# Differential attention inside a decoder layer: queries and keys transposed by VectorE in 32x32 blocks, and two of each head's steps in other slots

## What is computed

```python
h = x @ w_in                                   # all projections, q, k, v of both branches and the gates
dq, dk, dv, dz, db, da, aq, ak, av, ga, gb = jnp.split(h, split_at, axis=-1)
# differential attention, per head and block of 128 queries
s = einsum('bhmqd,bhmkd->bhmqk', qb, kb) * 64 ** -0.5 + alibi_bias     # m = 0, 1
p = softmax(s)
p_diff = p[:, :, 0] - lam * p[:, :, 1]
o = rms_norm(p_diff @ v, norm_w) * (1 - lambda_init)
```

## Time and profile before

| | us |
|---|---|
| median of 3 runs (lowest, highest) | 1954.68 (1954.41, 1956.05) |
| profiled execution, time | 1955.3 |
| its span in the profile | 1953.4 |
| TensorE busy | 1938.1 (99%) |
| VectorE busy | 1287.9 (66%) |
| ScalarE busy | 934.6 (48%) |

### The profile page before, as it was taken

The page is one execution under the profiler, slowest core; times in us unless marked ns, Lnnn a source line. Parts: engine busy times, 40 slices in busy tenths (PEclk is TensorE's granted clock), DMA queues, the critical chain, the costliest instruction groups (busy, mean ns, idle before and its releaser), DMA issues.

```text
span 1953.4 us, 33127 instructions
## 1 busy us (share of the span) xinstructions
PE 1938.1 (99%) x11260; PEld 1593.1 (82%) x11260; DVE 1287.9 (66%) x1873; ACT 934.6 (48%) x1286; POOL 43.1 (2%) x104
## 2 busy tenths in 40 slices
PE   9999999999999999999999999999999999999997
PEld 7788887888888888887888888788888888888886
DVE  7768577676557575757567656577775466664656
ACT  5555465554445555555544435644443444443442
POOL 0102010010100000000000000000000000000000
PEclk9999999999999999999999999999999999999999
DMA  7444444444554545454655676555555556555554
GB/s 259 159 141 152 153 140 142 151 152 140 173 183 163 182 161 182 158 183 156 199 190 197 212 238 212 172 191 196 194 192 195 191 194 192 192 195 192 195 191 173
DMA packets 98012, 353.19 MB, mean 181 GB/s; under 512 B 10832, under 2 KB 11120, under 8 KB 97776
## 3 DMA queue, kind: packets, MB, share of 16 engines
q1 hardware_dynamic: 97904, 351.65, 54.5%
HBM read 349.51 MB, written 2.10 MB: 180 GB/s over the span
## 4 chain that ended last, share of the span: by engine, by line
PE 96%; DVE 1%; ACT 1%; issue 1%; DMA 0%; SPq 0%; DVEq 0%; ACTq 0%
PE pg L393 88%; PE B L393 5%; DVE gates L1235 1%; PE B L491 0%; DMA raw<-in_weights 0%; PE B L649 0%; PE B L670 0%; PE B L582 0%; DVE wlo L1227 0%; ACT whi L827 0%; DVE cT L1235 0%; ACT hraw L1112 0%; PE B L523 0%; ACT gates L1100 0%; PE B L685 0%
## 5 line engine op out<-in xcount | busy, mean ns | idle before, releaser
L1227 DVE TENSOR_TENSOR wlo<-raw,whi 128x1024 fp32r<-128x1024 f32 (+1 forms) x640 | 778.3, 1220 | 520.1 <-ACT whi L827 502.9
L827 ACT ACTIVATE whi<-raw 128x1024 fp32r<-128x1024 f32 (+1 forms) x640 | 673.7, 1056 | 669.8 <-PE pg L393 661.1
L393 PE MATMUL pg<-whi,act_x 128*128 128x512 f32 x2960 | 957.5, 396 | 1.3 <-ACT whi L827 0.9
L393 PEld LDWEIGHTS pg<-whi,act_x 128*128 128x128 f32 x2960 | 555.9, 188 | 123.7 <-issue 8.5
L393 PE MATMUL pg<-wlo,act_x 128*128 128x512 f32 x1480 | 574.7, 390 | 0.0
L393 PE MATMUL pg<-whi,act_a 128*128 128x512 f32 x1632 | 505.0, 389 | 0.5 <-DVE act_a L1227 0.5
L393 PEld LDWEIGHTS pg<-whi,act_a 128*128 128x128 f32 x1632 | 306.4, 188 | 64.8 <-DVE act_a L1227 1.4
L393 PEld LDWEIGHTS pg<-wlo,act_x 128*128 128x128 f32 x1480 | 278.4, 188 | 52.9
L393 PE MATMUL pg<-wlo,act_a 128*128 128x512 f32 x816 | 317.5, 389 | 0.0
L393 PEld LDWEIGHTS pg<-wlo,act_a 128*128 128x128 f32 x816 | 153.2, 188 | 31.6
L393 PE MATMUL pg<-whi,act_b 128*128 128x512 f32 x512 | 158.5, 389 | 0.0
(11 more groups left out here) (227 smaller groups left out, 1025.7 us busy)
## 6 DMA issues: line engine op xcount, KB each, us to landing
raw<-in_weights SPq DMA_DIRECT2D x646, 512.0 KB, 3.8
gates<-in_ln_in SPq DMA_DIRECT2D x4, 512.0 KB, 6.4
gates<-in_ln_in SPq DMA_DIRECT2D x1, 2048.0 KB, 8.1
out<-gates SPq DMA_DIRECT2D x8, 256.0 KB, 2.7
raw<-in_weights SPq DMA_DIRECT2D x4, 256.0 KB, 4.5
cT<-in_xT SPq DMA_DIRECT2D x2, 512.0 KB, 7.6
qT<-in_xrow SPq DMA_DIRECT2D x2, 512.0 KB, 6.2
kT<-in_xrow SPq DMA_DIRECT2D x2, 512.0 KB, 5.4
```

The lines of the kernel that those rows point to most:

```text
L393: return nc.tensor.matmul(o, l, r, start=start, stop=stop)
L827: return nc.scalar.activation(o, i, ACT.Copy, scale=scale)
L1227: return V.tensor_tensor(o, a, b, op)
```

## The change

VectorE turns queries and keys: 16 block transposes for each, straight from `hraw` to `qT` or `kT` in SBUF, a few in each slot (4, 2, 4, 4, 2 in slots 19 to 23 for q and 3, 2, 3, 3, 3, 2 in slots 24 to 29 for k in a loop body; two in each of slots 8 to 23 in the first body). TensorE's transposes L649 and ScalarE's copies from `B[0]` are gone, and the factor 1/8 goes into the copy of q out of PSUM. The semaphore `dve_qkT` takes the place of `pe_qkT` and `act_qkT`: ScalarE's copy of the k group to `hraw` now waits until VectorE has turned the whole of q. The products with v move from s0+5 to slots 6, 12, 18 and 23, which for the first three heads is the slot of the next head's scores and ahead of them; the output transposes move from s0+7 to slots 10, 16, 22 and 25, which for the first three is the slot of the next head's probability transposes, behind them.

```diff
-DA_TURN = [(21, 23), (27, 29)]
-DA_TURN_FIRST = [(10, 12), (18, 20)]
+DA_TURN = [{19: 4, 20: 2, 21: 4, 22: 4, 23: 2}, {24: 3, 25: 2, 26: 3, 27: 3, 28: 3, 29: 2}]
+DA_TURN_FIRST = [{s: 2 for s in range(8, 16)}, {s: 2 for s in range(16, 24)}]
 HEAD_SLOTS = [0, 6, 12, 18]
+PV_SLOTS = [6, 12, 18, 23]
+OT2_SLOTS = [10, 16, 22, 25]
...
@@ TensorE
-            def da_turn(j, which, half, e, first):
...
-                        last = nc.tensor.transpose(B[0][:, i * SEQ + t * P:i * SEQ + (t + 1) * P],
-                                                   hraw[:, t, h * P:(h + 1) * P], ident)
-                last.then_inc(N["pe_qkT"], 1)
...
+            def da_mix(j, s):
+                for h, s0 in enumerate(HEAD_SLOTS):
+                    if s == PV_SLOTS[h]:
+                        pe.wait_ge(N["act_pT"], 1 + HB * j + h + 1)
+                        mm(B[3][:, 0:P], pT[:, 0:P], vda[:, 0, h * P:(h + 1) * P])
...
                 for h, s0 in enumerate(HEAD_SLOTS):
                     if s == s0:
-                        pe.wait_ge(N["act_qkT"], 1 + 4 * j + 4)
+                        pe.wait_ge(N["dve_qkT"], 1 + 2 * j + 2)
...
-                    if s == s0 + 5:
-                        pe.wait_ge(N["act_pT"], 1 + HB * j + h + 1)
...
-                    if s == s0 + 7:
-                        if h == HB - 1 and turning:
-                            pe.wait_ge(N["act_qkT"], 1 + 4 * (j + 1) + 2)
+                for h in range(HB):
+                    if s == OT2_SLOTS[h]:
                         pe.wait_ge(N["dve_oh2"], 1 + HB * j + h + 1)
...
@@ ScalarE
-            def rows_out(pair, dst, func=ACT.Copy):
+            def rows_out(pair, dst, func=ACT.Copy, scale=1.0):
...
                 if what == "q":
                     act.wait_ge(N["pe_conv"], 1 + 6 * NB)
-                    act.wait_ge(N["pe_qkT"], 1 + 4 * j)
-                    rows_out(i % 2, lambda t: hraw[:, t, :])
+                    act.wait_ge(N["dve_qkT"], 1 + 2 * j)
+                    rows_out(i % 2, lambda t: hraw[:, t, :], scale=CH ** -0.5)
                 if what == "k":
-                    act.wait_ge(N["pe_qkT"], 1 + 4 * j + 2)
+                    act.wait_ge(N["dve_qkT"], 1 + 2 * j + 1)
                     rows_out(i % 2, lambda t: hraw[:, t, :])
...
-            def da_turns(j, s, first):
...
-                        copy((qT, kT)[which][:, 2 * half:2 * half + 2, :],
-                             B[0][:, :].rearrange("p (h s) -> p h s", h=2), CH ** -0.5 if which == 0 else 1.0
-                             ).then_inc(N["act_qkT"], 1)
...
@@ VectorE
-                    if s == s0 + 5:
+                for h in range(HB):
+                    if s == PV_SLOTS[h]:
                         dve.wait_ge(N["act_oss"], 1 + HB * j + h + 1)
...
-                    if s == s0 + 7:
+                    if s == OT2_SLOTS[h]:
                         dve.wait_ge(N["act_oT2"], 1 + HB * j + h + 1)
...
+            def da_turns(j, s, first):
+                for which, slots in enumerate(DA_TURN_FIRST if first else DA_TURN):
+                    if s not in slots:
+                        continue
+                    at = sum(n for k, n in slots.items() if k < s)
+                    if at == 0:
+                        g = which if first else which + 1
+                        dve.wait_ge(evac[g % 2], 2 * NB + 2 * j + g // 2 + 1)
+                        dve.wait_ge(N["pe_s"], 1 + HB * j)
+                    out = blocks_out((qT, kT)[which][:, :, :])
+                    for i in range(at, at + slots[s]):
+                        a, b = divmod(i, 4)
+                        ins = V.transpose(out[b * SB:(b + 1) * SB, :, :, a, :], blocks_in[a * SB:(a + 1) * SB, :, :, b, :])
+                    if i == 15:
+                        ins.then_inc(N["dve_qkT"], 1)
...
             with dve.Fori(1, NB) as j:
-                body(N_DA + BODY * j, [chained("da_chain", DA_LINKS * (j - 1), da_mix, j - 1, DA_LINKS)])
+                body(N_DA + BODY * j, [chained("da_chain", DA_LINKS * (j - 1), da_mix, j - 1, DA_LINKS),
+                                       lambda s: da_turns(j, s, False)])
```

More of the change, by code:

```diff
@@ L637, in dn_scan @@
                     last.then_inc(N["pe_oT"], 1)
-            def da_turn(j, which, half, e, first):
[L641 to L648, removed]
-                        last = nc.tensor.transpose(B[0][:, i * SEQ + t * P:i * SEQ + (t + 1) * P],
-                                                   hraw[:, t, h * P:(h + 1) * P], ident)
-                last.then_inc(N["pe_qkT"], 1)
-            def da_mix(j, s, turning):
+            def da_mix(j, s):
[3 more added lines that the diff above has]
+                        mm(B[3][:, 0:P], pT[:, 0:P], vda[:, 0, h * P:(h + 1) * P])
+                        mm(B[3][:, P:2 * P], pT[:, P:2 * P], vda[:, 0, h * P:(h + 1) * P], True, False)
+                        mm(B[3][:, P:2 * P], pT[:, 2 * P:3 * P], vda[:, 1, h * P:(h + 1) * P], False, True
+                           ).then_inc(N["pe_pv"], 1)
                 for h, s0 in enumerate(HEAD_SLOTS):
                     if s == s0:
-                        pe.wait_ge(N["act_qkT"], 1 + 4 * j + 4)
+                        pe.wait_ge(N["dve_qkT"], 1 + 2 * j + 2)
                         pe.wait_ge(N["dve_s1"], 1 + HB * j + h)
@@ L716, in _ @@
                                               lambda s: dn_build(j, s)])
-            def da_turns(j, s, first):
[L719 to L725, removed]
+            body(N_DA, 2 * NB, act_x, [lambda s: dn_scan(NB - 1, s, True)])
             with pe.Fori(1, NB) as j:
-                body(N_DA + j * BODY, 2 * NB + 2 * j, act_x,
-                     [lambda s: da_mix(j - 1, s, True), lambda s: da_turns(j, s, False)])
-            body(N_GB, 4 * NB, act_x, [lambda s: da_mix(NB - 1, s, False)])
+                body(N_DA + j * BODY, 2 * NB + 2 * j, act_x, [lambda s: da_mix(j - 1, s)])
+            body(N_GB, 4 * NB, act_x, [lambda s: da_mix(NB - 1, s)])
             def first_up(n, g):
@@ L1050, in da_mix @@
                         last.then_inc(N["act_oss"], 1)
-                    if s == s0 + 7:
+                    if s == s0 + 4:
+                        act.wait_ge(N["pe_pT"], 1 + HB * j + h + 1)
+                        act.wait_ge(N["pe_pv"], 1 + HB * j + h)
+                        copy(pT[:, :], B[3][:, 0:3 * P]).then_inc(N["act_pT"], 1)
+                    if s == OT2_SLOTS[h]:
                         act.wait_ge(N["pe_oT2"], 1 + HB * j + h + 1)
@@ L1547, in da_mix, with blocks_out @@
                            ).then_inc(N["dve_oT2"], 1)
+            blocks_in = hraw[:, :, :].rearrange("p t (c b x) -> p t c b x", c=4, x=SB)
+            def blocks_out(dst):
+                return dst.rearrange("p c (t a x) -> p t c a x", t=TOK, x=SB)
+            def da_turns(j, s, first):
[13 more added lines that the diff above has]
+                        ins.then_inc(N["dve_qkT"], 1)
             body(N_DA, [chained("scan_chain", SCAN_LINKS * (NB - 1), dn_scan, NB - 1, SCAN_LINKS,
-                                alone=True)])
+                                alone=True), lambda s: da_turns(0, s, True)])
             with dve.Fori(1, NB) as j:
-                body(N_DA + BODY * j, [chained("da_chain", DA_LINKS * (j - 1), da_mix, j - 1, DA_LINKS)])
+                body(N_DA + BODY * j, [chained("da_chain", DA_LINKS * (j - 1), da_mix, j - 1, DA_LINKS),
+                                       lambda s: da_turns(j, s, False)])
             body(N_GB, [chained("da_chain", DA_LINKS * (NB - 1), da_mix, NB - 1, DA_LINKS)])
@@ L1561, in turn_rows @@
                 ins.then_inc(N["dve_mT"], 1)
-            blocks_in = hraw[:, :, :].rearrange("p t (c b x) -> p t c b x", c=4, x=SB)
-            blocks_out = turned.rearrange("p c (t a x) -> p t c a x", t=TOK, x=SB)
             def turn_blocks(cnt, s, place):
@@ L1574, in turn_blocks @@
                         a, b = divmod(i, 4)
-                        ins = V.transpose(blocks_out[b * SB:(b + 1) * SB, :, :, a, :],
+                        ins = V.transpose(blocks_out(turned)[b * SB:(b + 1) * SB, :, :, a, :],
                                           blocks_in[a * SB:(a + 1) * SB, :, :, b, :])
```

22 lines of the change are left out of this document (7 added, 15 removed).

## The result

| | before | changed |
|---|---|---|
| median, us | 1954.99 (1954.39 to 1956.05, 10 runs) | 1959.61 (1958.44 to 1960.74, 10 runs) |
| ratio | 1 | 1.0023, 95% interval 1.0013 to 1.0033 |
| profiled execution: time, span, mean clock | 1955.3, 1953.4, 0.998 | 1960.42, 1958.3, 0.997 |
| first scores of the four bodies, us | 565.77, 664.40, 763.02, 861.65 | 564.08, 664.68, 765.52, 866.52 |
| loop bodies, us | 98.63, 98.62, 98.63 | 100.60, 100.84, 101.00 |

A forecast was written before the change was run, and what follows sets the result against it. TensorE, busy 99% of the span, bounds the kernel. Loop bodies -1.85 - 0.2 + 4.1 = +2.05, three times +6.15; first body -1.85, last -0.2; together +4.1 gives 1958.8 us, range 1954.0 to 1963.0.

The forecast's parts named there:

- T: The moment in a loop body when the fourth head's scores (slot 18) are done; VectorE's queue is followed from there.
- Rival (a): VectorE has room in a loop body and all the added work hides: 1946.5; chance 0.10 for faster by over 0.2%.
- What leaves TensorE: In first and loop attention bodies, TensorE's dropped transposes of queries and keys save 1.85 us per body.
- Sharing: Products with v and output transposes beside the next head's steps save TensorE 0.03 to 0.04 us each, 0.2 per body.
- The price of a block: On VectorE, n block transposes in a group cost 0.16 + 0.445n us; 32 add about 17 us to a body.
- Lateness: TensorE waits because VectorE's work behind the fourth head's scores makes tile 27 late: 4.1 us per loop body.
- The foreseen waits: TensorE waits at slot 22 (0.3 us, probabilities), slot 25 (2.2, `oh`) and tile 27 (1.3), in each loop body.
- only the last of the waits counts: In a loop body, later TensorE waits take in the earlier delays, since VectorE's queue does not move with TensorE's.
- Cost zero for reloads, for ScalarE, and behind tile 27: Raw buffer reloads, ScalarE's lost copies and VectorE's 2.63 us per slot against 2.72 behind tile 27 add nothing.
- The clock stays at 1.00: TensorE's granted clock does not fall in the new pauses; leaving 1.00 was listed as a sign of being wrong.
- rival (c): TensorE's clock falls after the new pauses of each loop body, costing +8 to +16 us, around 1971; chance 0.04.

The follow-up runs named there:

- experiment 2: Changed kernel with only the third head's products with v a slot earlier, in slot 17 instead of 18; 1953.91 us.
- experiment 4: Changed kernel with every second query block transpose left out in the loop bodies, so it serves for time only; 1948.06 us.
- experiment 6: The respaced kernel: changed one with third products with v in slot 17, last output transpose in 26, query blocks 2, 4, 2, 4, 4 in slots 18 to 22; 1949.68 us.
- experiment 9: The written-out respaced kernel: that of experiment 6 with VectorE's loop over the three attention bodies written out; 1946.96 us.
- experiment 5: Kernel before, TensorE's transposes kept, only products with v and output transposes moved so four steps per body share a place; 1954.5 us.
- experiment 3: Changed kernel with the keys copied to a buffer of their own, so their copy doesn't wait for the query blocks; 1958.27 us.
- experiment 7: Changed kernel with only the query blocks moved, to 2, 4, 2, 4, 4 in slots 18 to 22; 1962.5 us.
- experiment 8: Changed kernel with only the last output transposes a slot later, in slot 26 instead of 25; 1966.65 us.
- experiment 10: Changed kernel with VectorE's loop over the three attention bodies written out; 1958.59 us.
- experiment 1: Changed kernel with products with v and output transposes back in their old slots, VectorE still turning queries and keys; 1959.01 us.
- experiment 11: Kernel before the change with VectorE's loop over the three attention bodies written out; 1954.93 us.

## Why the prediction was right, and where it was not

**The result and its mechanism.** Forecast 1958.8, measured 1959.61, inside the range; the ratio lies just past the line of 0.2% on the forecast's side, but its interval takes in both sides. The mechanism is shown by experiments 2 and 4: less work of VectorE between T and its last query block makes the body shorter, be it the third head's chain or half of the blocks. Experiments 2 and 6 show that its total load isn't the cost, since it is the same there. Rival (a) has fallen for this order of slots. For another order it is true: the written-out respaced kernel, at 1946.96, stands where (a) had put a change that hides (1946.5).

**What leaves TensorE: 1.85 per body.** The first body gave 1.69, or 1.6 as the average over the profiles. In the loop bodies the saving together with sharing is 98.63 - 96.55 = 2.08 when nothing waits (experiment 9, with five shared places), against 1.85 + 0.2 = 2.05. With the sixth place it would be an estimated 2.13.

**Sharing: 0.2 per body.** Four places gave 98.63 - 98.43 = 0.2 (experiment 5), so the six of the change are worth an estimated 0.3: a term that was too small by 0.1.

**The price of a block: 0.16 + 0.445n.** Groups of 4 and 2 took 1.78 and 0.88; the 0.12 ahead of a group came in only some places. The figure of one element per cycle for the transposing front end that the Trainium skill gives (Vector Engine (DVE) Microarchitecture Reference, section 3.8), an estimated 0.27 us for this shape, again doesn't describe the whole instruction: 0.445 in this kernel's row too. The row was right to decide. Only the total was added up wrongly: by these prices 32 blocks in eleven groups are 16.0 us and not about 17; nothing was built on it.

**Lateness 4.1 per loop body.** The first body, in which the clock stayed at 1.00, has 100.60 - 96.55 = 4.05, or 4.1 with the sixth shared place. The foreseen waits of 0.3, 2.2 and 1.3 came out at 0.4, 2.1 and 1.2. That the sum hits so closely is in part luck: with VectorE's loop written out the same body is 100.35, so the steps of the forecast are worth some 3.85, and 0.25 is the hole in the chain of `oh`, which it didn't hold. That only the last of the waits counts holds as long as the clock doesn't fall (experiments 3 and 7).

**Cost zero for reloads, for ScalarE, and behind tile 27.** No wait on a transfer is listed for TensorE. Landing took 4.0 us in place of 3.8 (3.7 to 4.2 over all kernels, with blocks and without), and ScalarE's waits for a reload grew from 8.0 us in 11 places to 18.8 in 17; none of them reached TensorE in a loop body.

**The clock stays at 1.00: wrong,** and by the prediction's own list a sign of being wrong. I gave rival (c) 0.04, because 2.2 us looked short beside the 8 us of the earlier trace rows, and expected a tile or two at the low level for it. Windows of the changed kernel's second loop body:

```profile
744.00:745.00 1.00, 0.58 (x4) 0.54 (x5) 0.96 (x3) 0.00 (x0) 0.00 (x0) 1.00 0.07 25
745.00:746.00 1.00, 1.00 (x6) 0.83 (x5) 0.29 (x1) 0.67 (x2) 0.00 (x0) 0.93 0.00 0
746.00:747.00 1.00, 1.00 (x4) 0.81 (x3) 0.00 (x0) 1.00 (x2) 0.00 (x0) 0.50 0.00 0
747.00:748.00 1.00, 1.00 (x4) 0.71 (x4) 0.61 (x1) 1.00 (x2) 0.00 (x0) 0.50 0.00 0
748.00:749.00 1.00, 1.00 (x4) 0.56 (x3) 0.99 (x3) 1.00 (x3) 0.00 (x0) 0.50 0.00 0
749.00:750.00 1.00, 1.00 (x6) 0.80 (x6) 0.97 (x3) 1.00 (x2) 0.00 (x0) 0.86 0.30 45
```

TensorE came back from a pause of 2.14 us at 744.42, and from about 745.9 it ran at half its clock for some 3.3 us, 1.7 us lost. It cost this kernel almost nothing, since TensorE would have waited 1.2 us at tile 27 anyhow (that wait is missing in this body, and the body is 0.24 longer than the first). So (c) was right as a mechanism and wrong in its price for this kernel; where no wait follows, the 1.7 us are paid in full (experiments 3, 7 and 8). The Trainium skill (TensorE: Matmul & The Clock Gate, Why this matters for your kernels) warns of idle gaps between bursts; this trace bears that out, with a pause as short as 2.1 us.

**What no step foresaw: VectorE's start of a body.** Its first split of the third loop body came 3.08 us after its last instruction, at 767.80, where the second had 1.97. Against the written-out kernel (experiment 10) the third body lost 0.64 (101.00 and 100.36), the first, with no late start, 0.25 (100.60 and 100.35). I had followed VectorE from slot 18 on alone and taken the start for unchanged. In the sum this 0.4, the 0.24 of the second body and the 0.25 of the hole stand against the larger saving and the slightly smaller lateness: terms that the forecast lacked came out about as large as its errors, and the total is closer than its parts.

## What to carry to other kernels

A busy share says whether work fits an engine, not whether it fits a place. Follow the receiving engine's queue from the last event that it must wait for to the first thing that others need from it; here 3 us of movable work in that stretch decided between 0.2% slower and, with the rest of the respacing, 0.3 to 0.4% faster. Move such work out of the stretch before giving up on the change, and add up small waits with care: a pause of TensorE of 2 us could bring its lower clock with it, one long pause cost more here than two short ones, and a wait right behind a pause hid that.

## What the runs showed of the hardware beside this

**Pauses and the clock.** In these traces, pauses of 0.7 to 1.6 us in the attention bodies brought no fall of the granted clock by themselves (eight in experiments 2, 6 and 8). Pauses of 1.9 to 2.2 us were in some cases: one of three in the changed kernel and in experiments 1, 3 and 10, two of three in experiment 7. Pauses of 3.5 us always were (three of three). After about 2 us the fall begins between 0 and 1.5 us after TensorE is back at work and lasts some 3.4 us; after 3.5 us it began 0.2 and 0.9 us before TensorE was back, and in the third case 1.1 us after, and lasted 3.4, 6.8 and 3.4 us. Why one body falls and its twin doesn't stayed open.

**The return of a loop.** VectorE's loop returns twice in a run, and its first split behind a return has to wait for ScalarE's rounding. In the kernels with loop and blocks it starts 0.5 us after that rounding when all goes well; in nine of 16 returns it started 1.1 to 3.4 us after it. It was one of the two returns in the changed kernel and in experiments 1 and 6, both in experiments 3, 7 and 8, and none in experiments 2 and 4. Without the blocks the split starts 0.1 us after the rounding, and with the loop written out at once (0.03). That it takes both the return and the blocks is shown by experiments 9 to 11.

The traces also say what VectorE waits for, though no experiment isolates it. They list a DMA queue, q14, that carries instructions. Its packets between 618 and 861 us, the stretch with both returns, in the changed kernel (packets, MB, share of the DMA engines):

```profile
q14 instruction: 11, 0.09, 0.1%
```

In the kernel before q14 has no packet in this stretch. In the respaced kernel one of them runs from 663.49 to 663.89, between the end of the rounding at 661.93 and the late split at 665.28. In all nine late cases the split follows the end of such a packet by 1.15 to 1.54 us, and at the seven other returns none starts sooner behind one either (1.34 to 1.75). So VectorE very likely reads instructions there, in a loop that without the blocks needs no reading. Why the packet comes late at one return and not at the next is open; the count of packets doesn't tell, since experiments 2 and 4, with no late start, have as many (39) as the others.
